# A streaming encoder step in which the second looped pass also makes the gates of the last tile

## The reference

```python
def _token_mixers(h, ...):                       # h = rms(x) * ln1_g
    cq, ckv, kpe, bq, bk, bv, iq, iw, ik, ga, gb = jnp.split(h @ w_in, offs, axis=-1)
    ...                                          # mixer A (MLA) gives o_a, mixer B (top-k sparse) gives o_b
    merged = jax.nn.sigmoid(ga) * (o_a @ w_o_a) + jax.nn.sigmoid(gb) * (o_b @ w_o_b)
    return merged @ w_out, new_rows

def _peer(h, wq, subkeys, u, v):                 # 8 heads, 128 x 128 experts, top 16 a head
    q = (t @ wq)...;  e, sc = top16 of the sums of two top-16 lists of q @ subkeys
    a = gelu(einsum('td,thkd->thk', t, u[e]))    # u[e], v[e]: 128 rows of 1024 for every token
    return einsum('thk,thkd->td', softmax(sc) * a, v[e])

x = x + token_mixers(rms(x, ln1_g));  x = x + peer(rms(x, ln2_g))
```

## Time and profile before

| | us |
|---|---|
| median of 3 runs | 1799.13 |
| lowest, highest | 1796.78, 1801.43 |
| profiled execution, its own time | 1796.99 |
| its span, first to last instruction | 1795.2 |
| PE busy | 1223.4 (68%) |
| DVE busy | 1310.8 (73%) |
| ACT busy | 579.7 (32%) |
| POOL busy | 526.2 (29%) |
| DMA, mean rate over the span | 388 GB/s |

### The profile page before, as it was taken

How to read it: one execution, slowest core, us unless ns; L and a number is a source line. 1 busy time by engine, 2 the same in 40 slices (tenths; PEclk the granted TensorE clock), 3 DMA queues, 4 the chain that set the end, 5 groups by cost and what they waited for, 6 DMA issues and landing times.

```text
span 1795.2 us, 26399 instructions
## 1 busy us (share of the span) xinstructions
PE 1223.4 (68%) x9056; PEld 679.3 (38%) x9056; DVE 1310.8 (73%) x3857; ACT 579.7 (32%) x1995; POOL 526.2 (29%) x569
## 2 busy tenths in 40 slices
PE   8989976677867575878877666679867343434343
PEld 3668532344535232444535223356535111111111
DVE  5662696989666676989666768998766878686754
ACT  2331134333423333334323334344423222222222
POOL 0200232333322223332322223232323333333332
PEclk9989889787988696897998697887999555555555
DMA  6238699999999999999999999999999999999997
GB/s 267 74 100 294 250 422 421 422 425 425 424 424 423 417 401 383 420 425 424 425 423 422 423 407 390 426 400 398 422 424 423 427 426 426 425 427 423 427 421 294
DMA packets 119381, 696.48 MB, mean 388 GB/s; under 512 B 17983, under 2 KB 21118, under 8 KB 49102
## 3 DMA queue, kind: packets, MB, share of 16 engines
q0 software_dynamic: 78848, 570.53, 76.0%
q1 hardware_dynamic: 36686, 121.83, 17.5%
q10 hardware_dynamic: 3712, 2.43, 0.4%
HBM read 691.65 MB, written 3.02 MB: 387 GB/s over the span
## 4 chain that ended last, share of the span: by engine, by line
DMA 35%; DVE 25%; PE 25%; issue 6%; ACT 3%; POOL 1%; ACTq 0%; DVEq 0%; SPq 0%; POOLq 0%
DMA rows<-in_peer_uv,index 26%; DVE rows L2657 11%; PE ps_v L1820 5%; DMA wch<-in_w_row 4%; PE ps_f L1559 4%; PE ps_f L1353 2%; PE ps_f L1574 2%; PE ps_h L1800 2%; DMA wch<-in_peer_wq 2%; DVE score L2333 1%; PE ps_f L1477 1%; PE ps_f L1653 1%; DVE best L2332 1%; DMA wch<-in_w_ukv 1%; PE ps_f L1437 1%
## 5 line engine op out<-in xcount | busy, mean ns | idle before, releaser
L2657 DVE CUSTOM_DVE_ANT_0 rows<-rows,ps_h 128x1024 f32<-128x1024 f32 x544 | 658.0, 1220 | 289.1 <-DMA rows<-in_peer_uv,index 236.3
L1330 POOL DMA_INDIRECT rows<-in_peer_uv,index x544 | 516.4, 949 | 1169.4 <-PE ps_v L1820 988.8
L1820 PE MATMUL ps_v<-rows,diag 128*32 128x256 f32 x4352 | 419.1, 500 | 432.0 <-ACT diag L2164 424.8
L1820 PEld LDWEIGHTS ps_v<-rows,diag 128*32 128x32 f32 x4352 | 124.2, 130 | 677.5 <-ACT diag L2164 561.7
L2155 ACT ACTIVATE tan<-arg 128x2 f32<-128x2 f32 x272 | 55.3, 203 | 799.2 <-DVE arg L2667 756.4
L2158 ACT ACTIVATE weight<-tan,lead 128x1 f32<-128x1 f32 x544 | 180.8, 379 | 9.1
L2164 ACT ACTIVATE diag<-sel,weight 128x32 f32<-128x32 f32 x544 | 140.9, 306 | 0.6 <-PE ps_v L1820 0.6
L1559 PEld LDWEIGHTS ps_f<-bufh,wch 128*128 128x128 f32 x768 | 103.7, 214 | 19.9 <-issue 17.8
L1559 PE MATMUL ps_f<-bufh,wch 128*128 128x128 f32 x768 | 109.7, 302 | 0.0
L1353 PE MATMUL ps_f<-wch,bufh 128*128 128x512 f32 (+1 forms) x192 | 81.9, 565 | 27.7 <-DMA wch<-in_w_row 26.7
L1653 PE MATMUL ps_f<-bufh,wch 128*128 128x128 f32 x384 | 52.1, 293 | 12.5 <-DMA wch<-in_peer_wq 12.3
(11 more groups left out here) (398 smaller groups left out, 1682.4 us busy)
## 6 DMA issues: line engine op xcount, KB each, us to landing
wch<-in_w_gate SPq DMA_DIRECT2D x60, 512.0 KB
wch<-in_w_row SPq DMA_DIRECT2D x36, 512.0 KB
wch<-in_w_o SPq DMA_DIRECT2D x32, 512.0 KB
wch<-in_w_out SPq DMA_DIRECT2D x24, 512.0 KB
wch<-in_peer_wq SPq DMA_DIRECT2D x24, 512.0 KB
rows<-in_peer_uv,index POOLq DMA_INDIRECT x544
w_tok<-in_w_tok SPq DMA_DIRECT2D x4, 1640.0 KB, 12.9
wch<-in_w_uq SPq DMA_DIRECT2D x6, 384.0 KB
```

What stands on the lines that cost most here:

```text
L1330: pool.indirect_dma_start(rows[c % RING][:, :, :].rearrange("p a d -> p (a d)"), None, io.peer_uv[:, :], at).then_inc(s_uv[c % RING], 16)
L1820: ins = nc.tensor.matmul(ps_v[GROUP * a:GROUP * (a + 1), :], diag[:, c % DRING, :], rows[c % RING][:, 1, QD * a:QD * (a + 1)], start=False ...
L2657: v.tensor_tensor_reduce(out=u, in0=u, in1=ps_h[:, :], scale=1.0, scalar=0.0, op0=ALU.mult, op1=ALU.add, accum_out=dots[:, c % KEEP:c % KE ...
```

## The change

The second looped pass also takes the x rows of the last tile: SP loads them to `oab` (idle then), DVE and PE make h of them ahead of the pass's own, and it is put at `h_pair[:, 1]`, a view whose second half is the buffer `hrows1`, 1024 numbers a partition, and whose first half is `bufh`. The gate matmuls of this pass then have a moving operand of 2 x 128 columns, and give the gates of both tiles at once. ACT writes the tanh of its own tile to `sg` as before, that of the last tile to one of four parts of `qh` (`ASIDE = 4`), and stores it to a DRAM tensor `kept` by a DMA on its own queue. In the third looped pass `gates_of` is empty: no gate load, no gate matmul, no tanh; SP loads `kept` back to `sg` in one 1 MB DMA, when the projection in `sg` has been turned and its stores have landed, and DVE waits for it in `merged`.

```diff
@@ step_work @@
+    if p == BOTH:
+        pe_head[-1] = DC * small
...
-        if 0 <= k < 6 * DC and k % 6 in (2, 4):
-            pe += DC * small
+        if 0 <= k < 6 * DC and k % 6 in (2, 4) and p <= BOTH:
+            pe += DC * (0.4 if p == BOTH else small)
@@ stream @@
+    def gate_width(p):
+        return width_of(p) + (P if p == BOTH else 0)
+    def gate_rows(p, k):
+        return m.h_pair[:, :, P * k:P * (k + 1)] if p == BOTH else h_of(p)[:, k, 0:width_of(p)]
+    MORE = PASSES[BOTH][0] - 1
+    def turn_of(i):
+        return i - 1 + (i > MORE)
+    def kept_at(j):
+        return qh[:, 2 * (j % ASIDE):2 * (j % ASIDE) + 2, :]
...
-             for j in (list(range(J_AT, V_AT + 1)) + list(range(K_AT)) if p
+             for j in (list(range(J_AT, V_AT + 1)) + list(range(Z_AT if p == BOTH + 1 else 0, K_AT)) if p
...
     def gates_of(p):
-        return range(0 if p else SOON, DC)
+        return range(DC if p == BOTH + 1 else 0 if p else SOON, DC)
@@ sync @@
+                    if p == BOTH:
+                        sp.wait_ge(s_ot, 2 * (i - 1))
+                        sp.dma_start(junk, io.x_prompt[P * (t + 1):P * (t + 2), :]).then_inc(s_more_x, 16)
                     sp.dma_start(tab, io.tabs[:, t, :]).then_inc(s_tab, 16)
...
-                    for n in range(WRING):
-                        load_gate(p, n)
+                    if p <= BOTH:
+                        for n in range(WRING):
+                            load_gate(p, n)
                     sp.wait_ge(s_norm, p)
...
-                for n in range(WRING + (0 if p else 2 * SOON), 2 * DC):
-                    load_gate(p, n)
+                if p == BOTH + 1:
+                    sp.wait_ge(s_pair, 3 * p)
+                    sp.wait_ge(s_qk, p)
+                    sp.wait_ge(s_new, 16 * 5 * p)
+                    for n in range(ASIDE):
+                        sp.wait_ge(s_kept[n], 16 * (DC // ASIDE))
+                    sp.dma_start(idle_sg, m.kept[:, :, :, :].rearrange("p j a k -> p (j a k)")).then_inc(s_back, 16)
+                else:
+                    for n in range(WRING + (0 if p else 2 * SOON), 2 * DC):
+                        load_gate(p, n)
@@ tensor @@
             def gate(p, j, a):
...
+                sums = gated(p)[:, a, :]
+                if p == BOTH:
+                    sums = sums.rearrange("p (t k) -> p t k", t=2)
                 for k in range(DC):
-                    ins = nc.tensor.matmul(gated(p)[:, a, :], w[:, k, :], h_of(p)[:, k, 0:n],
-                                           start=(k == 0), stop=(k == DC - 1))
+                    ins = nc.tensor.matmul(sums, w[:, k, :], gate_rows(p, k), start=(k == 0), stop=(k == DC - 1))
...
+                        if x == -1 and p == BOTH:
+                            turn_x(i, MORE)
@@ scalar, tanh_gates @@
+                if p == BOTH:
+                    nc.scalar.activation(sg_of(p)[:, :, j, :], gated(p)[:, :, 0:P], ACT.Tanh, scale=0.5)
+                    if j >= ASIDE:
+                        act.wait_ge(s_kept[j % ASIDE], 16 * (j // ASIDE))
+                    nc.scalar.activation(kept_at(j), gated(p)[:, :, P:2 * P], ACT.Tanh, scale=0.5).then_inc(s_sig, 1)
+                    act.wait_ge(s_sig, gates_through(p, j))
+                    act.dma_start(m.kept[:, j, :, :], kept_at(j)).then_inc(s_kept[j % ASIDE], 16)
+                    return
...
+                        if x == -3 and p == BOTH:
+                            root_x(MORE)
@@ vector @@
+            def more_sum():
+                dve.wait_ge(s_more_x, 16)
+                x_squares(junk)
...
+            def more_columns(i):
+                dve.wait_ge(s_h, first_block(i - 1))
+                columns_out(m.h_pair[:, 1, 0:D].rearrange("p (c k) -> p c k", c=DC), MORE)
...
-                if p or j >= SOON:
+                if p == BOTH + 1:
+                    dve.wait_ge(s_back, 16)
+                elif p or j >= SOON:
                     dve.wait_ge(s_sig, gates_through(p, j))
...
+                        if x == -4 and p == BOTH:
+                            more_sum()
+                        if x == -2 and p == BOTH:
+                            x_scale(p, junk, MORE)
+                        if x == 0 and p == BOTH:
+                            more_columns(i)
@@ hybrid_step @@
+    m.kept = nc.dram_tensor("kept", [P, DC, 2, P], F32).ap()
```

62 lines of the change are left out of this document (41 added, 21 removed).

## The result

The changed kernel takes 1810.27 us (median of 5 runs, 1806.31 to 1825.44), the kernel before beside it 1799.13 us (1794.68 to 1801.43); the ratio is 1.0081, with a 95% interval of 1.0057 to 1.0104. The forecast was 1792.4 us. The change makes the kernel slower, by about 11 us in the medians, where 6.7 us less was forecast.

The account below looks back on a forecast made before the run. Transfers were taken as the bound, in balance with DVE in one third-pass stretch. Third pass -15.1 and second +8.4 gave -6.7 us: 1788.5 for the span, 1792.4 for the median, range 1784.5 to 1801.5.

Parts of the forecast that it names:

- What the removed loads leave idle: Third pass's units: DVE binds 1122.4 to 1219.2, most freed transfer time is used for early gathers; idle grows 5.5 us.
- the third pass's half: Third pass: transfers -18.3, idle +5.5, small losses recovered -2.3, together -15.1 us.
- The ring: Third pass: gathered-row slots let up to 4 columns, 10 us, be gathered ahead and used where DVE waited 29.3 us.
- Rival C: Third pass's DVE-bound stretch keeps 96.8 us, only one or two columns carried; +0.5 us, 1799.6; chance 0.27.
- PE gets emptier: Third pass, 1219.2 to 1288.3: PE loses 15.64 us of gates, small transfer losses mostly go; -2.3 us with early w_o loads.
- The rule I cited: Second pass's units: a fuller PE would be granted more than 0.85; lowered the slower rival's chance, not the sum.
- The transfers' bytes: Whole kernel: q1 about 8 MB less, q10 and the load from `kept` 1 MB each; transfers together -13.9 us.
- the rest: Second pass beyond PE's width: +4.4 us for x tile and stores, +1.0 for DVE, PE and ACT at its start.
- PE's term: Second pass's units: wider gates add 33 us of PE work, mostly hidden; charged 3.0 us (0 to 33).
- Rival D: PE becomes the bound of the second pass's units; +6.8 us, 1805.9, or +23 with all 33 visible; chance 0.13.

Follow-up runs that it names:

- e2: Kernel before, third pass without gate loads and gates, 1 MB of gate weights loaded instead, last tile's gates left out; 1796.32 us, ratio 0.9993.
- e12: The change with the planner counting a second-pass gate 8.0 instead of 3.2, so wide gates stand farther apart; 1822.04 us, ratio 1.0147.
- e6: The change with the third pass's 16 gate loads put back, each used by one small product nobody reads; 1815.29 us, ratio 1.0112.
- e3: The change with the planner still counting the third pass's missing gates, so steps keep their old columns; 1810.91 us, ratio 1.0070.
- e8: The change with DVE's time counted double in the planner's due times for the third pass; 1824.05 us, ratio 1.0121.
- e9: The change with half of the keys left out of the third pass's choice, cutting DVE work; 1806.83 us, ratio 1.0039.
- e1: The change's second pass with the old third pass, which makes its own gates; stored gates unused; 1809.39 us, ratio 1.0055.
- e5: The change's second pass with gates only 128 columns wide, and the old third pass; stored gates unused; 1802.18 us, ratio 1.0016.
- e10: The kernel before with half of the keys left out of the third pass's choice, cutting DVE work; 1797.54 us, ratio 0.9991.
- e14: The change with 32 unread identity products of 256 columns added in the third pass; 1810.46 us, ratio 1.0059.
- e11: Kernel before, third pass without gate loads and gates, plus 128 unread identity products of 16 columns; 1846.56 us, ratio 1.0262.
- e13: Kernel before, third pass without gate loads and gates, plus 32 unread identity products of 256 columns; 1803.40 us, ratio 1.0019.
- e4: The change with the planner still counting the third pass's gates and 128 unread identity products at their old places; 1805.94 us, ratio 1.0031.
- e7: Kernel before, third pass without gate loads and gates, plus 128 unread identity products of 128 columns, not counted by the planner; 1804.59 us, ratio 1.0032.

## Why the prediction was wrong

**The step that failed is "What the removed loads leave idle".** It charged 5.5 us for idle transfers and took another 2.3 off. The runs put the third pass's half at -2.6 us by e2's trace and -1.7 by its median, where -15.1 stood: of the 18.3 us of transfers some 16 went idle. The units show it best: 165.9 us before, 167.0, 167.1 and 166.8 in the change, e2 and e12, with 18.2 us of loads fewer in them. (In the change's trace the pass stands at +4.8, 3.3 of it given back behind it. e12 has 390.3 for the pass; the 7 us between them lie outside the units and are scatter or the state in which the second pass leaves the buffers.) Three things in that step were wrong.
- Its place was too small. I counted DVE as the bound in 1122.4 to 1219.2 only, since in the window behind it DVE is busy 52.19 of 69.10 us. But that window kept its length too (65.8 us), and e6 shows both with room for more transfers (rate up by 25 and 22 GB/s when the loads came back). What sets the pace in the second is not shown; PE (54.40 of 65.80 us) and the steps that hand over between PE, ACT and DVE are my guess. The step's own sum also had a slip: it took 16.5 us to be free without the gates, though gathers and loads, priced 90.7 us, already stood against a DMA share of 1.00 over 96.80, so no more than the loads' 10.4 us were new room there.
- The ring did not carry four columns' worth. I read DVE's 29.3 us of waits for rows as a place where rows gathered early are used. After the change 22.5 us of them are left, so some 7 us were carried at the most, 2.6 of them behind the units, and the pass's other parts took those back. Rival C had this mechanism, with 6 to 8.5 us for the pass more than I took; it too was too mild.
- "PE gets emptier" was booked as a gain of 2.3 us. The units' first window was granted 0.57 to 0.63 in the traces with no gates and nothing large in their place (the change, e2, e3, e6, e8, e9, e12), and 0.79 to 0.83 in those with gates (before, e1, e5, e10). In that window PE's remaining work took longer than the old work with the gates (78.83 against 71.49 us). That this alone costs the kernel time is not shown (e14 lifts the clock and has the same median); where the lower clock goes on into the next window, that window took 16 us more (e9, 82.0 against 65.8). The rule I cited, that activity releases the throttle (the Trainium skill, "TensorE: Matmul & The Clock Gate", Part 1), speaks of this case and I used it only for the second pass: there the clock went from 0.86 to 0.88, next to nothing, and in the third pass it fell from 0.83 to 0.58, so the trace agrees where I did not look. It does not agree if activity is read as PE's busy time: e11's windows are the busiest of all and have 0.57.

**What held.** The transfers' bytes are as forecast. The second pass cost 8.4 us in the trace, just the forecast, but that is luck in part: its two halves, 5 for PE's width and 4 for the rest (e5; 7 and 3 by the ratios), stand beside 3.0 and 5.4 forecast, so PE's term was too small and the rest too large. PE's added busy time in the pass was 21.9 us, not 33 or more. A record of the 256-column gate took 65.7 / 256 = 0.257 us of busy time, 0.271 estimated from the earlier trace rows:

```profile
L1607 PE MATMUL ps_f<-hpair,wch 128*128 128x256 f32 x256 | 65.7, 414 | 0.0
```

Rival D, PE as the bound of the second pass's units, was half right: PE reached 86% of the 160.0 us there, not the 90% that was to show it, and the rate was 400 GB/s instead of 424. DVE waited for scores, 13.2 us where the trace of before has 0.3:

```profile
DVE logit L2429 <- PE ps_f L1483: 13.2, 5, 5.8
```

The 8 stores were not tried apart; their share is somewhere in the 3 to 4 us of "the rest". They landed in 7.8 us in the median:

```profile
kept<-qh ACTq DMA_DIRECT2D x8, 128.0 KB, 7.8
```

The 160 last columns took 402.1 us instead of 405.4. The forecast had them unchanged, and in the 17 traces, none of which edits them, they take 399.6 to 405.4, so 3.3 us there are scatter.

**What stays open.** Why the lower clock goes on in some runs and not in others I cannot say. Nor is it settled whether half clock in the first window alone costs anything: e2 and e13 have 0.58 and 0.74 there and take 101.60 and 100.80 us. What bounds the units' second window was not tried. And e4 gained 5 us over e3 by products that cost e7 8 us; that the planner had kept room for them in e4 is likely, but it was not tried apart.

## What to carry to other kernels

Before bytes are priced as time, ask in each stretch what happens when they are gone: where DMA share is 1.00 and an engine at 90% or more at once, the two are in balance, and little more than that engine's own slack can be gained. The cheapest test is the one of e2: leave the loads and what uses them out, with a wrong output, and time it before building the rest; it would have shown 2 us instead of 15. Adding loads, as e6 does, tells only of the kernel they are added to: it cost 5 us in the change, where DMA share was 0.94, and says nothing of a stretch at 1.00. Work taken off TensorE can lower the clock of what stays on it (0.83 to 0.58 here), and where the lower level lasts likely the pace too, so a kernel with less matrix work is not always the one that waits less for it.

## What the runs showed of the hardware

PE's busy share did not say which clock it was granted. In e11, 94% busy over 220.8 us (208.33 us of it) with 128 added products of 16 columns, it kept 0.57; in e7, with products of 128 columns, 84% busy, it had 0.79 and 0.93. The added narrow records, at the lower clock, took longer than the wide ones at the higher (busy time and mean ns, first e11, then e7):

```profile
L1792 PE MATMUL ps_f<-bufh,ident 128*128 128x16 f32 x247 | 51.6, 358 | 0.0
```

```profile
L1792 PE MATMUL ps_f<-bufh,ident 128*128 128x128 f32 x248 | 36.5, 308 | 0.0
```

Runs of one program (e9) fell into two groups with means of 1799.7 and 1813.1 us, and in e9 the mean granted clock of a run, 0.773 or more against 0.770 or less, told the two apart; the change's own runs did not divide so.
